# Attention of a transformer block on TensorE, VectorE and ScalarE: the units between the projection matmuls go by twos

## The reference

```
qkv = x @ w_qkv                                   # (1024, 3072)
for each row r of 16 and each head of 64 columns:
    s  = q_r @ k_b.T (q scaled by 1/8)            # k_b, v_b: the 8 rows around r
    s  = where(column in window of 16, s + bias, -inf)
    pr = softmax(s);  out_r = pr @ v_b
mix = out @ w_o
...
ple = sigmoid(x1 @ w_ple_gate) * (p @ w_ple_proj)
```

## Time and profile before

| | us |
|---|---|
| median of three runs | 1228.02 (1227.34 to 1228.05) |
| the profiled execution | 1228.21 |
| its span, from first to last instruction | 1226.4 |
| PE busy | 1213.7 |
| DVE busy | 879.2 |
| ACT busy | 593.7 |

### The profile page before, as it was taken

One profiled execution on the slowest core, in us unless ns is written; L12 is line 12 of the kernel. 1 busy time (PEld: TensorE's weight loads), 2 busy tenths in 40 slices (PEclk: granted clock), 3 DMA queues, 4 the chain that ended last, 5 costly groups with the idle time before them and its releaser, 6 DMA issues.

```text
span 1226.4 us, 17904 instructions
## 1 busy us (share of the span) xinstructions
PE 1213.7 (99%) x5820; PEld 1018.7 (83%) x5820; DVE 879.2 (72%) x1732; ACT 593.7 (48%) x1145; POOL 127.4 (10%) x81
## 2 busy tenths in 40 slices
PE   8999999999999999999999999999999999999997
PEld 7888888888888788888888888888888888888886
DVE  3677777777777857769777777777764575588786
ACT  3565655655556843244544444444553433333671
POOL 0212222122123523200000000000000000000000
PEclk9999999999999999999999999999999999999999
DMA  8323223212233757783566465565669776768533
GB/s 219 78 71 79 58 72 90 55 55 72 57 106 80 278 150 225 203 283 135 197 206 232 169 235 204 191 235 178 223 235 381 278 274 230 252 238 310 195 103 103
DMA packets 162694, 215.61 MB, mean 176 GB/s; under 512 B 11456, under 2 KB 91200, under 8 KB 162240
## 3 DMA queue, kind: packets, MB, share of 16 engines
q1 hardware_dynamic: 162624, 214.72, 53.9%
HBM read 147.57 MB, written 58.90 MB: 168 GB/s over the span
## 4 chain that ended last, share of the span: by engine, by line
PE 94%; DVE 2%; issue 2%; ACT 1%; DMA 1%; SPq 0%; DVEq 0%; ACTq 0%
PE bank L2724 25%; PE bank L2692 25%; PE bank L1178 18%; PE bank L1325 7%; PE bank L2648 6%; PE bank L1279 3%; PE bank L1258 3%; PE bank L1237 3%; PE bank L1213 2%; PE bank L257 1%; PE bank L1229 1%; DMA weight_raw<-in_na_w_qkv 1%; PE bank L1192 1%; DVE probabilities L1080 1%; DVE prob_T_lo L1052 1%
## 5 line engine op out<-in xcount | busy, mean ns | idle before, releaser
L868 ACT ACTIVATE probabilities<-negated_scores,negated_max 128x384 f32<-128x384 f32 (+1 forms) x128 | 75.7, 591 | 136.2 <-DVE negated_max L1071 135.7
L1178 PE MATMUL bank<-act_T_hi,w_qkv_hi 128*128 128x512 f32 x336 | 133.7, 398 | 0.0
L1178 PE MATMUL bank<-act_T_lo,w_qkv_hi 128*128 128x512 f32 x336 | 133.5, 397 | 0.0
L1178 PE MATMUL bank<-act_T_hi,w_qkv_lo 128*128 128x512 f32 x336 | 131.8, 392 | 0.0
L2692 PE MATMUL bank<-x_combination,weight_parts 128*128 128x512 f32 x504 | 118.5, 389 | 0.0
L1052 DVE TENSOR_TENSOR prob_T_lo<-bank,prob_T_hi 128x256 fp32r<-128x256 f32 (+2 forms) x160 | 69.0, 448 | 60.0 <-ACT prob_T_hi L859 58.4
L2692 PEld LDWEIGHTS bank<-x_combination,weight_parts 128*128 128x128 f32 x504 | 94.6, 188 | 19.6
L748 POOL TENSOR_TENSOR w_qkv_lo<-weight_raw,w_qkv_hi 128x1024 fp32r<-128x1024 f32 x21 | 50.3, 2394 | 282.6 <-ACT w_qkv_hi L814 282.6
L2692 PE MATMUL bank<-act_T_hi,weight_parts 128*128 128x512 f32 x240 | 77.3, 389 | 0.0
L1080 DVE TENSOR_SCALAR probabilities<-probabilities,total_reciprocal 128x384 f32<-128x384 f32 (+1 forms) x128 | 73.8, 577 | 4.6
L2052 ACT ACTIVATE hidden_staging<-hidden_staging 128x512 f32<-128x512 f32 x48 | 30.4, 632 | 95.0 <-DVE hidden_staging L2389 95.0
(11 more groups left out here) (262 smaller groups left out, 2815.5 us busy)
## 6 DMA issues: line engine op xcount, KB each, us to landing
hidden_combinations<-hidden_staging SPq DMA_DIRECT2D x112, 256.0 KB, 2.7
w_ff_in<-in_w_ff SPq DMA_DIRECT2D x27, 1024.0 KB, 7.8
weight_raw<-in_w_ff SPq DMA_DIRECT2D x25, 1024.0 KB, 5.7
weight_raw<-hidden_combinations SPq DMA_DIRECT2D x14, 1024.0 KB, 5.5
hidden_in<-hidden_combinations SPq DMA_DIRECT2D x14, 1024.0 KB, 5.7
weight_raw<-in_na_w_qkv SPq DMA_DIRECT2D x21, 512.0 KB, 4.4
bias_in<-rpb_rows SPq DMA_DIRECT2D x256, 6.0 KB
attention_T<-out_T SPq DMA_DIRECT2D x8, 512.0 KB, 3.1
```

The source lines that it names most:

```text
L868: nc.scalar.activation(prob[:, u % 4, 0:n], score[:, u % 2, 0:n], ACT.Exp, scale=-1.0, bias=nmax[:, u % 4:u % 4 + 1], accum_out=total[:, u ...
L1178: mm = nc.tensor.matmul(proj_ps[gi % 2][:, :], w[wp][:, (par + kind) % 2, k, :], S.act[ap][:, k, t * HALF:(t + 1) * HALF], start=(i == 0), ...
```

## The change

In the pairs with projections the step functions of PE, DVE and ACT take two units at a time, in odd steps; even steps hold projection matmuls alone. `two_units(s, lag)` gives the two units of a stage. Scores of units s − 1 and s, normalisation of s − 3 and s − 2, transposition of s − 5 and s − 4, weighing of s − 7 and s − 6 all fall in the odd step s; steps 18 and 20 take what would be due in 19 and later. On PE the order within a step is now projection, scores, `turn_v`, weighing, transposition. The first 18 steps have 120 projection matmuls (6 or 7 each), steps 18 and 19 have 12 each. `EVAC_STEP` came to 4, 7, 10, 14, 17 and 20 before. The evacuation steps and the steps of weight splits are given as constants. The last pair's code moves to `last_body` as it was. In pair 6 the rows of `p` go two and two (steps 17, 17, 18, 18) through banks 2 and 3 alone; rows n = 2 and 3 wait for the low part of row n − 2.

```diff
-EVAC_STEP = [(GROUP_MMS * (gi + 1) - 1) * FILL_STEPS // FILL + 1 for gi in range(6)]
-V_TURN_STEP = (4, 7)
+LONG_STEPS, LONG_MMS = 2, 12
+EVAC_STEP = (2, 6, 10, 14, 17, 19)
+V_TURN_STEP = (3, 7)
+K_SPLIT_STEP, Q_SPLIT_STEP, V_SPLIT_STEP = 1, 7, 15
 PROJ_STEP = (17, 18)
-P_TURN_STEP = (17, 17, 17, 18)
+P_TURN_STEP = (17, 17, 18, 18)
...
+def fill_to(s):
+    short = FILL_STEPS - LONG_STEPS
+    return (FILL - LONG_STEPS * LONG_MMS) * s // short if s <= short else FILL - LONG_MMS * (FILL_STEPS - s)
+def two_units(s, lag):
+    return [u for u in (s - 1 - lag, s - lag) if s % 2 and 0 <= u < UNITS]
+def scored_at(s):
+    return two_units(s, 0)
+def normalised_at(s):
+    return two_units(s, 2)
+def turned_at(s):
+    return [UNITS - 2, UNITS - 1] if s == FILL_STEPS - 2 else two_units(s, 4) if s < FILL_STEPS - 2 else []
+def weighed_at(s):
+    if s >= FILL_STEPS - 2:
+        return {FILL_STEPS - 2: [UNITS - 4, UNITS - 3], FILL_STEPS: [UNITS - 2, UNITS - 1]}.get(s, [])
+    return two_units(s, 6)
...
         def p_bank(n):
-            return S.ps[(2, 3, 0, 3)[n]]
+            return S.ps[2 + n % 2]
...
@@ scalar, body @@
+                for s in range(STEPS + 1):
+                    if s in V_TURN_STEP:
+                        turned_v(1 - par, j + 1, V_TURN_STEP.index(s))
+                    for u in turned_at(s):
+                        turned_tile(j, u)
+                    for u in scored_at(s):
+                        softmax_exp(j, u)
+                    for h, b in out_evac_at(s):
+                        out_low(j, h, b)
+                    if not loads:
+                        proj_work(s)
+                    if s in EVAC_STEP[2:]:
+                        evac(1 - par, j + 1, EVAC_STEP.index(s))
...
@@ vector, body @@
+                for s in range(STEPS + 1):
+                    for u in normalised_at(s):
+                        normalise(j, u)
+                    for u in scored_at(s):
+                        add_bias(j, u)
+                    if s in V_TURN_STEP:
+                        turned_v(1 - par, j + 1, V_TURN_STEP.index(s))
+                    for u in turned_at(s):
+                        turned_tile(j, u)
+                    for h, b in out_evac_at(s):
+                        out_sum(j, h, b)
+                    if not loads:
                         for n in p_turns_at(s - 1):
                             dve.wait_ge(p_hi, n + 1)
...
+                    if s in EVAC_STEP:
                         evac(1 - par, j + 1, EVAC_STEP.index(s))
...
@@ tensor, turn_p_rows @@
                 if n < 2:
                     pe.wait_ge(score_done, UNITS * LAST + (n + 1))
-                elif n == 2:
-                    pe.wait_ge(proj_free, 6 * PAIRS + 1)
-                else:
-                    pe.wait_ge(p_lo, 2)
+                else:
+                    pe.wait_ge(p_lo, n - 1)
...
@@ tensor, body @@
+                for s in range(STEPS):
+                    if s < FILL_STEPS:
+                        project(1 - par, j + 1, fill_to(s), fill_to(s + 1))
+                    for u in scored_at(s):
+                        scores(par, j, u)
+                    if s in V_TURN_STEP:
+                        turn_v(j + 1, V_TURN_STEP.index(s))
+                    for u in weighed_at(s):
+                        for h, k in pv_units_at(u + WEIGH):
+                            weigh_v(par, j, h, k)
+                    for u in turned_at(s):
+                        turn_p(j, u)
+                    if not loads:
+                        for n in p_turns_at(s):
+                            turn_p_rows(n)
```

More of the change, by code:

```diff
@@ L933, in _, with last_body @@
             first_evac(Q_, 1)
-            def body(j, par, more, loads):
+            def last_body(j):
                 for s in range(STEPS + 1):
-                    if not more and 0 < s <= 2 * GROUPS:
+                    if 0 < s <= 2 * GROUPS:
                         embedded(s - 1)
@@ L941, in body @@
                         turned_tile(j, s - PARTS)
-                    if not more and s < UNITS:
+                    if s < UNITS:
                         softmax_exp(j, s)
@@ L945, in body @@
                         out_low(j, h, b)
-                    if more and s in EVAC_STEP[2:]:
-                        evac(1 - par, j + 1, EVAC_STEP.index(s))
[L948 to L958, removed]
+                    last_pair_work(s)
+            def body(j, par, more, loads):
+                if not more:
+                    last_body(j)
+                    return
+                for s in range(STEPS + 1):
[10 more added lines that the diff above has]
+                    if s in EVAC_STEP[2:]:
+                        evac(1 - par, j + 1, EVAC_STEP.index(s))
+                    if s == K_SPLIT_STEP:
                         split((par + 1 + K_) % 2, K_, 16 * j + 32)
-                    if s == EVAC_STEP[1] + 2:
+                    if s == Q_SPLIT_STEP:
                         act.wait_ge(proj_full, 6 * j + (6 + 2))
                         split((par + 1 + Q_) % 2, Q_, 16 * j + 32)
-                    if loads and s == EVAC_STEP[3] + 4:
+                    if loads and s == V_SPLIT_STEP:
                         act.wait_ge(proj_full, 6 * j + (6 + 4))
@@ L1118, in body @@
                         out_sum(j, h, b)
-                    if more and s - 1 in V_TURN_STEP:
-                        turned_v(1 - par, j + 1, V_TURN_STEP.index(s - 1))
-                    if more and not loads:
+                    if s == LAST_SPLIT_STEP:
+                        for t in range(2):
+                            dve.wait_ge(o_hi, t + 1)
+                            nc.vector.tensor_tensor(early_part(1, t)[:, LAST, :], o_st[:, t * P:(t + 1) * P],
+                                                    early_part(0, t)[:, LAST, :].bitcast(F32), ALU.subtract).then_inc(o_lo, 1)
+            def body(j, par, more, loads):
+                if not more:
+                    last_body(j)
+                    return
+                for s in range(STEPS + 1):
[10 more added lines that the diff above has]
+                    if not loads:
                         for n in p_turns_at(s - 1):
@@ L1255, in scores @@
                 if isinstance(j, int) and j == LAST and u < 2:
[L1256 removed]
+                    pe.wait_ge(p_lo, u + 3)
                 for part in range(2):
@@ L1307, in embed @@
                     pe.wait_ge(proj_w_lo, PC)
+                    pe.wait_ge(proj_free, 6 * PAIRS + 1)
                 elif u == 1:
@@ L1371, in _, with last_body @@
                     turn_first_v(0 if kind == V_ else 1)
-            def body(j, par, more, loads):
+            def last_body(j, par):
                 for s in range(STEPS):
-                    if more and s < FILL_STEPS:
-                        project(1 - par, j + 1, FILL * s // FILL_STEPS, FILL * (s + 1) // FILL_STEPS)
                     if s < UNITS:
                         scores(par, j, s)
-                    if not more and s < 2 * GROUPS:
+                    if s < 2 * GROUPS:
                         embed(s)
@@ L1384, in body @@
                         weigh_v(par, j, h, k)
-                    if more and s in V_TURN_STEP:
-                        turn_v(j + 1, V_TURN_STEP.index(s))
-                    if more and not loads:
+                    if s in EARLY_PRODUCTS:
+                        done = sum(EARLY_PRODUCTS[i] for i in EARLY_PRODUCTS if i < s)
+                        early_products(0, done, done + EARLY_PRODUCTS[s])
+            def body(j, par, more, loads):
+                if not more:
+                    last_body(j, par)
+                    return
+                for s in range(STEPS):
[4 more added lines that the diff above has]
+                    if s in V_TURN_STEP:
+                        turn_v(j + 1, V_TURN_STEP.index(s))
+                    for u in weighed_at(s):
[4 more added lines that the diff above has]
+                    if not loads:
                         for n in p_turns_at(s):
                             turn_p_rows(n)
-                    if not more and s in EARLY_PRODUCTS:
-                        done = sum(EARLY_PRODUCTS[i] for i in EARLY_PRODUCTS if i < s)
-                        early_products(0, done, done + EARLY_PRODUCTS[s])
             pairs_loop(pe, body)
```

## The result

The changed kernel takes 1234.12 us (median of 6 runs, 1233.61 to 1234.67) against 1228.03: a ratio of 1.0051, with a 95% interval of 1.0041 to 1.0061. Its profiled execution took 1234.67, with a span of 1232.9 (before 1228.21 and 1226.4). One of the six executions of the kernel before took 1518.82 us, far above the other five (1227.14 to 1228.18), and is left out of the ratio. The forecast was 1231.9, "slower"; the range holds the time, but 2.2 us are missing: two errors of my terms, 2.2 and 1.7 us, point the same way, and a smaller one of 0.6 hides part of them.

The account below looks back on a forecast made before the run. PE was taken to bound the kernel, busy 1213.7 of 1226.4 us. 1228.21 - 2.2 + 3.5 + 2.6 = 1232.1, set to a median of 1231.9 as the profiled execution stood 0.19 above the median; range 1227.9 to 1235.0.

Parts of the forecast that it names:

- Term 1: Loop pairs on PE: eleven interruptions instead of twenty save 0.315 us a pair, -2.2 us over 7 pairs.
- The friction of 0.7 a pair: Loop pair on PE: 49.50 us against 48.8 without friction, the rest laid to 20 interruptions at 0.035 us each.
- the six that I called undisturbed: Six projection matmuls on PE, 329.43 to 330.79, taken as the pace without friction: 1.36 us, 0.227 each.
- Rival C: Projection matmuls: the pace of 0.231 is their own, not the interruption's, so no saving there; 1234.1 us, chance 0.10.
- Term 2: Step 17: PE newly waits for DVE's low parts of units 10 and 11, 0.5 us a pair, +3.5 us.
- 18 hops: The chain over ACT and DVE summed for step 17, giving unit 11's low part at 8.63 us.
- Term 3: Pair 6: p's row 2 waits 3.05 us for row 0's low part, an old 0.6 wait goes; +2.6 us.
- rival D: Pair 6: PE's clock falls in the hole, step 19's 12 matmuls at half speed cost 2.7 us; 1234.6, chance 0.05.
- row 3's 0.13: Pair 6, step 18: p's row 3 makes PE wait a further 0.13 us for DVE's next low part.
- `turn_v` in step 3: PE's wait for DVE's copy after V's last matmul: 1.37 us of cover against 1.22, hidden with 0.15 to spare.

Follow-up runs that it names:

- kernel 3: Changed kernel with p's rows copied in the step of their transposition, K's second evacuation in step 15 and V's weight split in step 17: 1227.07 us, ratio 0.9993.
- experiment 6: kernel 3 with a step's transpositions ahead of its weighing on PE, the order of the kernel before: 1226.54 us, ratio 0.9990.
- kernel 7: kernel 3 with uneven runs of 7, 20, 7, 20, 7, 20, 7, 20, 12, 12, 12 projection matmuls and K's second evacuation in step 14: 1227.15 us.
- 8: kernel 3 with the edits of experiment 6 and kernel 7 together: 1226.55 us, ratio 0.9989.
- experiment 2: Changed kernel with the evacuation of K's second half in step 15 instead of 14: 1239.8 us, ratio 1.0093.
- kernel 5: Changed kernel with ACT's second split of w_proj moved behind its copies of p's rows: 1233.42 us, ratio 1.0046.
- 2b: Changed kernel with K's second evacuation in step 15 instead of 14 and V's weight split in step 17 instead of 15: 1232.16 us, ratio 1.0033.

## Why the prediction came out as it did

**Term 1, fewer interruptions: the step that failed.** I put it at −2.2 us, 0.315 a pair, and it is 0: without its new waits the changed order takes 49.52 a pair, as before. The friction of 0.7 a pair was read rightly, but it doesn't go by the number of interruptions. The failed step is the product "nine interruptions fewer by 0.035", which takes the price of an interruption to be the same whatever it holds and however long the run behind it. Against steady pitches of 0.2267, 0.171, 0.117 and 0.109 us for 512, 384, 256 and 128 columns, half of the friction stands in places 2 to 10 of the runs: 0.35 us over twenty runs before, 0.37 over eleven in kernel 3. So an interruption cost 0.017 there and costs 0.033 now. The other half stands at the short matmuls and the change-overs, and stayed as well: 0.39 before, 0.36 to 0.37 in kernels 3, 6, 7 and 8.

One reason for the doubled price is shown: the disturbance lasts up to ten matmuls (2.3 us), and the old runs had seven or eight, which cut it short; in kernel 7, four runs cut to seven again take 0.04 us a pair away. Cutting alone doesn't give the old 0.35, though: twenty runs at 0.033 − 0.010 would have 0.46 (an estimate). Some old interruptions disturb hardly anything: three of the twenty runs of pair 5 are steady from the second place on. What decides where in its ten places the disturbance begins, no run here settles, and that the two sums come out alike is chance. I had seen seven disturbed matmuls in a run of seven, and took the end of the run for the end of the disturbance. And the six that I called undisturbed stand right behind an interruption too, one with four weighing matmuls behind its transpositions. Here is their run in the kernel before, whose later part is in the earlier trace rows:

```profile
328.28 0.49 PE L1237 MATMUL bank<-identity,probabilities 128*128 128x128 f32 x3
328.52 0.42 PE L1279 MATMUL bank<-prob_T_hi,v_hi_lo 128*128 128x384 f32 x1
...
329.20 0.39 PE L1178 MATMUL bank<-act_T_hi,w_qkv_hi 128*128 128x512 f32 x1
```

The change turned that order round, so that every run but two followed transpositions directly; experiment 6 prices this at 0.09 a pair. Rival C gave term 1 the right size with a wrong cause: the slow pace goes with the interruption, since places 11 and later are steady. That its 1234.1 is the measured time is luck: it has no fall of the clock, and 0.6 us too much for the waits.

**Term 2, the wait in step 17: right, 0.42 for 0.5.** Place and cause are as forecast. With zero at 231.05, the last transposition of unit 9, DVE's low part of unit 10 begins at 7.33 (I had 7.49), PE would come at 7.80 (7.76), and unit 11 is weighed at 8.46 (8.67 with the restart). In 18 hops the sum was off by 0.2 at most. Over seven pairs the term is 2.9, not 3.5.

**Term 3, the rows of p: right for the hole, 3.05 for 3.05**, but pair 6 lost more than the hole, since **rival D happened with it**. I had given it 0.05 and 2.7 us. The clock fell and stayed down for 3.4 us, and half speed in 3.4 us can't cost more than 1.7: it cost 1.67. The 12 matmuls that I had let go at half speed need 5.4 us for it. In experiment 2 the clock stayed down for 6.8 us behind a hole as long, and there eight transpositions and ten matmuls took 5.96 instead of 3.2: 2.8, my price. The trace agrees with the rule that the prediction took from the Trainium skill ("TensorE: Matmul & The Clock Gate", "The HAM clock gate"), that gaps between bursts of matmuls can throttle the clock: 0.51 over the 3.50 us from 398.90. The chance was too low, for the only row that bore on it said that 5 us were enough, and it didn't exclude 3.

**The sum again.** 0 + 2.9 + (3.05 + 1.67 − 0.59) = 7.0 us, where the seven pairs differ by 6.9 and the medians by 6.1; single executions of one kernel scatter by about 0.5. Predicted were −2.2 + 3.5 + 2.6 = 3.9. The term that failed and the clock add 3.9; the shorter wait takes 0.6 back, and row 3's 0.13, which doesn't show beside the slowed transpositions, the rest. That the median came out within the range owes something to luck: a term that should have saved 2.2 us saved nothing, a loss of 1.7 wasn't in the sum, and the range was wide enough for both. `turn_v` in step 3 stayed hidden in the loop, as forecast.

## What to carry to other kernels

Before you count what fewer interruptions save, see in the trace how long the pace stays disturbed behind one, and compare that with the runs that you have and will have; if the old runs are shorter than the disturbance, merging them may save nothing, as here. A hole of two or three microseconds on PE is to be priced at its length and the clock's share after it, here 1.4 to 2.8 us. When an instruction on DVE is moved, look at what of GpSimd's work it will then stand beside.

## What the runs showed of the hardware

- Behind most interruptions the projection matmuls (128 x 512, 0.2267 us apart when steady) begin late by up to 9 ns each, from the second place on, in an irregular but repeating order over ten places, 0.04 us in all where the whole order is met, and from there on not at all (39 distances in a pair of kernel 7, their sum within 0.003 us of none). It needs no transposition: four score matmuls bring it too. With the transpositions ahead of the weighing it is 0.27 a pair, otherwise 0.37 (kernels 6 and 3). Why wasn't found.
- The granted clock fell once for each hole, but not at one point of it: in the changed kernel 0.35 us and in kernel 5 0.16 us after PE had begun again, in 2b 0.42 and in 2 0.93 before. Counted from PE's last matmul ahead of the hole, it fell 2.0 to 3.2 us later. At the ends of the eleven traced executions, where no matmul follows, the clock fell 2.2 to 5.2 us after PE's last. It came back after 3.4 us, in kernel 2 after 6.8. The cost of the same hole of 3.05 thus differed: 1.67, 1.44 (2b) and 2.8 (2).
- A normalisation of 128 x 384 on DVE took 2.13 us beside GpSimd's 2.40 us `tensor_tensor` in kernel 2 and 2.31 to 2.32 in the loop of the kernel before; its median is 0.42. It ended about 0.2 us behind GpSimd's instruction both times.
